# Three feed-forwards rewritten by Strassen's scheme: seven half-size products per pair of weight tiles

## The chip, the core and the metric

The kernel runs on one core of a Trainium2 chip. The time is the device time of the whole program in microseconds (us). Three runs of the kernel before took 4400.33, 4402.57 and 4403.73 us; the median is 4402.57 us.

The engines are called as in the profile: PE is TensorE (the matmuls), DVE is VectorE, ACT is ScalarE, POOL is GpSimd, SP is SyncE, which here only issues DMAs. SBUF is the on-chip memory, PSUM the eight banks that PE writes (one bank holds 128 partitions x 512 fp32), DRAM the chip's large memory.

## The reference

Three blocks work on one sequence of 1024 tokens with 1024 channels. Each has a mixer (recurrences and convolutions, not touched by this change), an output projection, and a feed-forward, all in fp32:

```python
# block 1 (block 3 has the same feed-forward): 4096 hidden channels
h = h + y @ w_out
m = rmsnorm(h, norm_mlp_g) @ w_mlp_up            # 1024 -> 4096
h = h + square(relu(m)) @ w_mlp_down             # 4096 -> 1024
# block 2: 2816 hidden channels, gated
h = h + (silu(m @ w_gate) * (m @ w_up)) @ w_down
```

## The kernel before

Activations lie transposed, channels on the 128 partitions and the 1024 tokens along the free dimension. So `h` is 8 tiles of 128 x 1024, a weight matrix is cut into output tiles of 128 columns, and a hidden layer of 4096 channels is 32 tiles of 128 x 1024 (2816 channels are 22).

**A product in three parts.** PE multiplies in a reduced fp32 form, so each operand is split into an upper part and the rest: `hi` is the rounded copy (made by ACT, `split_hi`, L185) and `lo = x - hi` (made by POOL, `split_lo`, L191, for weights; by DVE for activations). Each product is hi·hi + hi·lo + lo·hi: three matmuls per 128 x 128 piece of weight and 512 tokens. `product` (L220 to L222) makes one output tile: 8 pieces of the contraction x 2 halves of the tokens x 3 = 48 matmuls into two PSUM banks.

**A feed-forward** (`back`, L508) starts with the 8 output tiles of the mixer's projection, whose results are added to `h` (L739), while the norm of the sum is made. It then walks over groups of 8 hidden tiles (`walk`): 8 tiles up, then 8 partial products down, added to `h` at L720. For the up tiles DVE takes the result out of PSUM (L709), scales it by the inverse norm `c_inv` (L712), squares it (L713), and splits it into `pair` (L686, L687), where the down products read it. In block 2 a gate tile and an up tile make one hidden tile (L694 to L702, ACT's Silu at L595). Nothing of the hidden layer goes to DRAM. Loops (`Fori`) run the groups on every engine.

**What sets the order.** Every engine runs its own list of instructions in order; semaphores tie them together. Two weight buffers take turns (`b` = 0, 1): SP loads a tile of 512 KB into `raw` when POOL has split the last one, ACT makes `whi` when PE has finished the product that used the old one, POOL makes `wlo`, PE starts. Tiles of a product use PSUM banks 0 and 1 or 4 and 5.

The function that the change rewrites is `back`, with its helpers `tail_scalar`, `tail_vector` and `sums_of`; `back_half` calls it three times, with `groups` = [(4, 8)] for blocks 1 and 3 and [(2, 8), (1, 6)] for block 2.

Of the kernel before, what the change touches and what calls it, by code (L numbers as in the profile page):

```python
# [15 lines left out]
P = 128  # L16
# [131 lines left out]
MIDDLE = ("m_summed", "m_logged", "m_root", "m_upper", "m_lower", "m_sq_a", "m_tot_a")  # L148
# [106 lines left out]
def next_norm(c, u, gain, off, second=None, of="n"):  # L255

    t = Shared()
    t.of = of
    t.c, t.u, t.gain, t.off, t.second = c, u, gain, off, second
    return t  # L260


def sums_of(pe, s, g, c, how, of="n"):

    for m in range(1 if how == "one" else 2):
        for j in range(2):
            mm = pe.matmul(s.psum[:, 2 + 4 * m + j, :], g.ones[:, :], c.tot[m][:, j * 512:j * 512 + 512], start=True,
                           stop=True)
        mm.then_inc(s[f"{of}_summed"], 1)
# [45 lines left out]


def tail_scalar(act, s, g, t, k):

    h = g.h[:, k, t.off:t.off + SEQ]
    act.wait_ge(s.free[k % 2], t.before + k // 2 + 2)  # L320
    if t.u is not None:
        act.activation(t.u[0][:, k, 0:SEQ], h, ACT.Copy, scale=t.gain(k)).then_inc(s[t.of + "_upper"], 1)
    bufs = len(t.buf_a)
    if k > bufs:
        act.wait_ge(s[t.of + "_tot_a"], k - bufs)
    act.activation(t.c.tot[0][:, 0:SEQ] if k == 0 else t.buf_a[k % bufs][:, 0:SEQ], h, ACT.Square)\
       .then_inc(s[t.of + "_sq_a"], 1)
    if t.second is not None:
        if k > 1:
            act.wait_ge(s[t.of + "_tot_b"], k - 1)  # L330
        act.activation(t.c.tot[1][:, 0:SEQ] if k == 0 else t.buf_b[:, 0:SEQ], h, ACT.Square, scale=t.second(k))\
           .then_inc(s[t.of + "_sq_b"], 1)


def tail_vector(dve, s, g, t, k):

    h = g.h[:, k, t.off:t.off + SEQ]
    if t.u is not None:
        dve.wait_ge(s[t.of + "_upper"], k + 1)
        dve.scalar_tensor_tensor(t.u[1][:, k, 0:SEQ], h, t.gain(k), t.u[0][:, k, 0:SEQ].bitcast(F32), ALU.mult,  # L340
                                 ALU.subtract).then_inc(s[t.of + "_lower"], 1)
    if k == 0:
        return
    sums = [("_sq_a", "_tot_a", t.c.tot[0], t.buf_a[k % len(t.buf_a)])]
    if t.second is not None:
        sums.append(("_sq_b", "_tot_b", t.c.tot[1], t.buf_b))
    for sq, tot, x, buf in sums:
        dve.wait_ge(s[t.of + sq], k + 1)
        if k > 1:
            dve.wait_ge(s[t.of + tot], k - 1)  # L350
        dve.tensor_tensor(x[:, 0:SEQ], x[:, 0:SEQ], buf[:, 0:SEQ], ALU.add).then_inc(s[t.of + tot], 1)
# [156 lines left out]
def back(nc, name, g, c, W, Wup, Wdown, groups, gated, off, middle, end, then=None, early=None, restore=None, ready=0):  # L508
# [11 lines left out]
    with stage(nc, name, *DENSE, *MIDDLE) as s:  # L520
        weight_buffers(s, c)
        xhi, xlo = x
        sq = s.sb("sq", [P, T])
        silu = c.tot[1][:, 0:T] if gated else None
        inv = sliced(g.inv[:, 0:T], T)
        middle.buf_a, middle.before = [c.inv, sq], 0
        end.buf_a, end.buf_b, end.before = [sq], c.inv, total - KD // 2

        def walk(eng, do_up, do_down, skip=0, last_down=None):

            before, tile = outs, 0
            for gi, (many, kt) in enumerate(groups):
                ups = kt if gated else kt // 2
                per = ups + KD // 2

                def one(o, skip=0, final=False):
                    with eng.Fori(0, ups - skip) as j:
                        do_up(j + skip, o * per + before + j + skip, o * kt + tile, kt, o)
                    if final:
                        for j in range(KD // 2):  # L540
                            last_down(j, o * per + before + ups + j, o * kt + tile, kt, o)
                    else:
                        with eng.Fori(0, KD // 2) as j:
                            do_down(j, o * per + before + ups + j, o * kt + tile, kt, o)

                lo, hi = 0, many
                peel = gi == len(groups) - 1 and last_down is not None
                if gi == 0 and skip:
                    one(0, skip)
                    lo = 1  # L550
                if peel:
                    hi -= 1
                if hi - lo > 1:
                    with eng.Fori(0, hi - lo) as o:
                        one(o + lo)
                elif hi - lo == 1:
                    one(lo)
                if peel:
                    one(many - 1, final=True)
                before += many * per  # L560
                tile += many * kt

        with nc.Block() as block:
            @block.sync
            def _(sp):
                def do_up(j, it, tile, kt, o):
                    for b in range(2):
                        at = tile * (2 * P if gated else P) + j * (2 * P) + b * P
                        load_tile(sp, s, b, it, up[:, :, ds(at, P)], KD)

                def do_down(j, it, tile, kt, o):
                    for b in range(2):
                        load_tile(sp, s, b, it, down[:, ds(tile, kt), ds(j * (2 * P) + b * P, P)], kt)

                for it in range(ready, KD):
# [4 lines left out]
                    if it == (1 if early is None else 3) and restore is not None:  # L580
                        sp.dma_start(g.h[:, :, off:off + SEQ], restore).then_inc(s["spilled"], 16)
                for b in range(2):
                    load_tile(sp, s, b, outs, first_up(b), KD)
                walk(sp, do_up, do_down, skip=1)
                if then is not None:
                    for n in range(4):
                        load_tile(sp, s, n % 2, total + n // 2, then(n), KD)
                    for b in range(2):
                        sp.wait_ge(s.landed[b], 16 * total + 32)

            @block.scalar
            def _(act):
                def gate(j, it, tile):
                    act.wait_ge(s["free0"], it + 2)
                    act.activation(silu, silu, ACT.Silu).then_inc(s["silu0"], 1)  # L595

                def do_up(j, it, tile, kt, o):
                    for b in range(2):
                        split_hi(act, s, b, it, KD)
                    if gated:  # L600
                        gate(j, it, tile)

                def do_down(j, it, tile, kt, o):
                    for b in range(2):
                        split_hi(act, s, b, it, kt)

                def last_down(j, it, tile, kt, o):
                    for b in range(2):
                        split_hi(act, s, b, it, kt)
                        if j:  # L610
                            tail_scalar(act, s, g, end, 2 * j - 2 + b)
# [10 lines left out]
                roots_of(act, s, c, "one", "m")  # L622
                if gated:
                    gate(0, outs, 0)
                walk(act, do_up, do_down, skip=1, last_down=last_down)
                tail_scalar(act, s, g, end, KD - 2)
                if then is not None:
                    split_hi(act, s, 0, total, KD)
                tail_scalar(act, s, g, end, KD - 1)
                if then is not None:  # L630
                    split_hi(act, s, 1, total, KD)
# [3404 lines left out]
```

## Time and profile before

| | us |
|---|---|
| median of three runs | 4402.57 |
| span of the profiled execution, first to last instruction | 4393.7 |
| what the runs take beyond that span | 8.9 |
| PE busy in the span | 3927.2 |
| DVE busy | 2089.7 |
| ACT busy | 1119.0 |
| POOL busy | 869.4 |
| DMA, mean of 73 GB/s | 319.75 MB |

No separate time is given for the profiled execution, so the median stands for its span with what lies around it. A PE matmul counts as busy for 0.39 us though the next one starts 0.23 us later, so PE's busy share says only where it had no work; how fast it goes is read from the count of matmuls in a window. The feed-forwards of blocks 1, 2 and 3 lie at about 515 to 1215, 2150 to 2870 and 3675 to 4370 us of the span.

### The profile page before, as it was taken

To read this page: it belongs to the slowest core of one execution; us is meant where nothing else is said; L and a number is where in the kernel's file an instruction comes from. 1 tells how busy PE (TensorE), PEld (TensorE's weight loads), DVE (VectorE), ACT (ScalarE), POOL (GpSimd) and SP (SyncE) were. 2 spreads that over 40 slices of the span, in tenths; PEclk is the share of its full clock that TensorE was granted. 3 is DMA by queue.
4 is the path that set the end of the run, shared out by engine and by line. 5 is a ranking of instruction groups with operands and counts; after the bars stand their busy time and mean duration, and the time that the engine had idled before them with its cause. 6 is when DMAs were issued, how large, how long until landed. Compare 5 with 4: busy or idle time off the path is not lost. (4 is left out here: it accounts for less than half of the span.)

```text
span 4393.7 us, 47463 instructions
## 1 busy us (share of the span) xinstructions
PE 3927.2 (89%) x18690; PEld 3275.1 (75%) x18690; DVE 2089.7 (48%) x2012; ACT 1119.0 (25%) x1368; POOL 869.4 (20%) x653
## 2 busy tenths in 40 slices
PE   9965999999989986767999999999943979999997
PEld 8953888888878776655888888878733958888886
DVE  3677445254544556365331322444768545253353
ACT  2503200000222233244211111243154552000001
POOL 1110222222222210200222222222220512222221
PEclk9987999999999998878999999999967989999998
DMA  3310111111133322442111111122272531111111
GB/s 131 103 45 23 46 51 49 48 48 48 48 130 110 117 80 46 120 156 67 46 50 48 48 48 48 48 82 91 88 177 39 158 126 48 48 48 48 48 50 60
DMA packets 446784, 319.75 MB, mean 73 GB/s; under 512 B 100181, under 2 KB 411989, under 8 KB 446649
## 3 DMA queue, kind: packets, MB, share of 16 engines
q1 hardware_dynamic: 437288, 283.72, 22.0%
q10 hardware_dynamic: 9360, 34.21, 2.0%
q8 instruction: 86, 1.41, 0.1%
q14 instruction: 50, 0.40, 0.0%
HBM read 245.22 MB, written 72.66 MB: 72 GB/s over the span
## 5 line engine op out<-in xcount | busy, mean ns | idle before, releaser
L191 POOL TENSOR_TENSOR c_wlo<-c_raw,c_whi 128x1024 fp32r<-128x1024 f32 (+1 forms) x169 | 409.4, 2423 | 1457.9 <-ACT c_whi L185 1457.9
L220 PE MATMUL c_acc<-c_hi,c_whi 128*128 128x512 f32 x1616 | 633.6, 392 | 0.6 <-POOL c_wlo L191 0.6
L221 PE MATMUL c_acc<-c_lo,c_whi 128*128 128x512 f32 x1616 | 629.2, 389 | 0.0
L222 PE MATMUL c_acc<-c_hi,c_wlo 128*128 128x512 f32 x1616 | 629.2, 389 | 0.0
L191 POOL TENSOR_TENSOR w_wlo<-w_raw,w_whi 128x1024 fp32r<-128x1024 f32 x116 | 291.6, 2514 | 1163.6 <-ACT w_whi L185 1163.6
L220 PE MATMUL c_acc<-pair,c_whi 128*128 128x512 f32 x1120 | 438.1, 391 | 45.6 <-POOL c_wlo L191 45.6
L185 ACT ACTIVATE c_whi<-c_raw 128x1024 fp32r<-128x1024 f32 (+1 forms) x169 | 177.1, 1048 | 1112.5 <-PE c_acc L222 1109.3
L221 PE MATMUL c_acc<-pair,c_whi 128*128 128x512 f32 x1120 | 437.5, 391 | 0.0
L222 PE MATMUL c_acc<-pair,c_wlo 128*128 128x512 f32 x1120 | 437.4, 391 | 0.0
L220 PE MATMUL c_acc<-c_hi,w_whi 128*128 128x512 f32 x1024 | 405.5, 396 | 12.4 <-POOL w_wlo L191 12.4
L221 PE MATMUL c_acc<-c_lo,w_whi 128*128 128x512 f32 x1024 | 399.7, 390 | 0.0
L222 PE MATMUL c_acc<-c_hi,w_wlo 128*128 128x512 f32 x1024 | 399.5, 390 | 0.0
L220 PE MATMUL c_acc<-pair,w_whi 128*128 128x512 f32 (+2 forms) x1024 | 377.4, 369 | 20.6 <-POOLq L165 20.6
L221 PE MATMUL c_acc<-pair,w_whi 128*128 128x512 f32 (+2 forms) x1024 | 373.8, 365 | 0.0
L222 PE MATMUL c_acc<-pair,w_wlo 128*128 128x512 f32 (+2 forms) x1024 | 373.6, 365 | 0.0
L185 ACT ACTIVATE w_whi<-w_raw 128x1024 fp32r<-128x1024 f32 x116 | 122.9, 1059 | 911.3 <-PE c_acc L222 877.6
L220 PEld LDWEIGHTS c_acc<-c_hi,c_whi 128*128 128x128 f32 x1616 | 303.7, 188 | 66.4 <-issue 3.0
L221 PEld LDWEIGHTS c_acc<-c_lo,c_whi 128*128 128x128 f32 x1616 | 303.6, 188 | 64.7 <-issue 2.2
L222 PEld LDWEIGHTS c_acc<-c_hi,c_wlo 128*128 128x128 f32 x1616 | 303.6, 188 | 63.4
L720 DVE TENSOR_TENSOR h<-h,c_acc 128x1024 f32 x64 | 78.2, 1222 | 566.0 <-PE c_acc L222 566.0
L220 PEld LDWEIGHTS c_acc<-pair,c_whi 128*128 128x128 f32 x1120 | 211.4, 189 | 91.2 <-POOL c_wlo L191 47.3
L221 PEld LDWEIGHTS c_acc<-pair,c_whi 128*128 128x128 f32 x1120 | 211.5, 189 | 44.0
(592 smaller groups left out, 5858.7 us busy)
## 6 DMA issues: line engine op xcount, KB each, us to landing
c_raw<-in_w_ff SPq DMA_DIRECT2D x64, 512.0 KB, 4.0
proj<-c_tot ACTq DMA_DIRECT2D x49, 512.0 KB, 2.6
w_raw<-in_w_in SPq DMA_DIRECT2D x48, 512.0 KB, 4.4
c_raw<-in_w_gu SPq DMA_DIRECT2D x44, 512.0 KB, 3.8
w_raw<-in_w_mlp_up SPq DMA_DIRECT2D x32, 512.0 KB, 4.0
w_raw<-in_w_mlp_down SPq DMA_DIRECT2D x32, 512.0 KB, 4.0
h<-proj SPq DMA_DIRECT2D x25, 512.0 KB, 5.7
c_raw<-in_w_in SPq DMA_DIRECT2D x25, 512.0 KB, 4.0
```

The source lines that it names most:

```text
L185: act.activation(s.whi[b][:, 0:kt, :], raw[:, 0:kt, :], ACT.Copy).then_inc(s.hi[b], 1)
L191: pool.tensor_tensor(s.wlo[b][:, 0:kt, :], raw[:, 0:kt, :], s.whi[b][:, 0:kt, :].bitcast(F32), ALU.subtract).then_inc(s.lo[b], 1)
L220: pe.matmul(out, s.whi[b][:, k, :], x_hi, start=(k == 0), stop=False)
L221: pe.matmul(out, s.whi[b][:, k, :], x_lo, start=False, stop=False)
L222: mm = pe.matmul(out, s.wlo[b][:, k, :], x_hi, start=False, stop=(k == kt - 1))
L720: dve.tensor_tensor(h, h, flat(s.psum[:, 4 * b:4 * b + 4, :], T), ALU.add)\
```

## The change

The scheme, in Winograd's form, takes two weight tiles A (cut into quarters: two halves of the contraction, two output tiles) and two halves of the tokens, and makes four output quarters from seven products of half the contraction instead of eight. The seven weight factors are A11, S2, S3, S1, A12, S4, A22 with sums S1 to S4 made by DVE per pair (`weight_sum`); the seven activation operands are three quarters as they are and four sums (T). One *unit* is seven *products* of 12 matmuls (4 pieces of the contraction x 3 parts, 512 tokens each), so 84 matmuls where 96 stood. The results are combined as they leave PSUM: `r1` is the first product, `u2` = r1 + the second, `u3` = u2 + the third, and the quarters C11, C12, C21, C22 from those and from the sums in the banks.

- The feed-forward runs in two passes: all the up units, then all the down units. The first pair of up tiles is still made by plain products (96 matmuls). Blocks 1 and 3 then have 15 up and 16 down units; block 2 has 21 up units (each a gate and an up tile) and 12 down units, the last four with 3 pieces of contraction in place of 4 (63 matmuls).
- Between the passes the hidden layer lies in DRAM, as seven operands per pair of tiles (`hidden`, 7 stores of 256 KB per pair). DVE makes the three sums (`sums_of_hidden`, L978 to L984), SP issues the stores (L608). Before DVE overwrites the place of C22 in the next tile it waits for all seven stores (`kept`).
- The down pass works in chunks of 4 pairs of hidden tiles (four units each). The seven operands of a chunk, 1 MB each, are loaded over the old ones as soon as these are done with, then split by ACT (L755) and DVE (L1102), at the places listed in `REFILL`.
- Weights are split per product: four slots of 128 x 512, ACT at L643, POOL behind it. A pair of weight tiles is loaded as two DMAs of 512 KB with rows of 1 KB.
- The loops are written out, and the ends of the feed-forward (squares and sums for the next norm) are placed among the last four units.

The core of the diff (the engine is the word ahead of each wait: `sp`, `act`, `pool`, `pe`, `dve`; `n` is the unit, `i` the product in it, `r` its place in the order):

```diff
+FACTOR = ("A11", "S2", "S3", "S1", "A12", "S4", "A22")
+BANK = (0, 1, 2, 3, 0, 3, 2)
+REFILL = (3, 4, 6, 8, 9, 11, 12)
...
+            for i in range(7):
+                at = -4 if i == 0 and fetched[nth] else REFILL[i]
+                refill_at.setdefault(divmod(7 * n + at, 7), []).append((nth, i))
...
+                        if r == 2 and n <= NA and (not gated or n % 2):
+                            sp.wait_ge(s["tee"], 4 * pair + 4)
+                            for i in range(7):
+                                sp.dma_start(hidden[i, pair], stored[i]).then_inc(s["kept"], 16)
...
+                        if nth is not None and not (r == 0 and fetched[nth]) and not (r == 6 and nth == 0):
+                            sp.wait_ge(s["fin"], 7 * n + r + 1)
+                            refill(nth, r)
...
+                def split_factor(q):
+                    if q >= 4:
+                        act.wait_ge(s["fin"], q - 3)
...
+                    act.activation(slots[q % 4][:, 0:depth(n), :], factor(n, i), ACT.Copy).then_inc(s["phi"], 1)
...
+                        if q + 4 < 7 * N:
+                            split_factor(q + 4)
...
+                        for nth, i in refill_at.get((n, r), ()):
+                            act.wait_ge(s[f"op{i}"], 16 * nth + 16)
+                            act.activation(hi[:, 0:kk, :], F(lo[:, 0:kk, :]), ACT.Copy).then_inc(s["op_hi"], 1)
...
+                    pool.wait_ge(s["phi"], q + 1)
+                    pool.tensor_tensor(slot[:, 4:4 + kk, :], factor(n, i), F(slot[:, 0:kk, :]), ALU.subtract)\
+                        .then_inc(s["plo"], 1)
...
+                    if i == 4:
+                        pe.wait_ge(s["first"], n + 1)
+                    elif i == 5:
+                        pe.wait_ge(s["c22"], n + 1)
+                    elif i == 6:
+                        pe.wait_ge(s["u3"], n + 1)
...
+                    if begins(n):
+                        pe.wait_ge(s["op_lo"], 7 * chunk(n) + i + 1)
+                    for k in range(kk):
+                        pe.matmul(out, slot[:, k, :], hi[:, k, :], start=fresh and k == 0, stop=False,
+                        pe.matmul(out, slot[:, k, :], lo[:, k, :], start=False, stop=False, skip_group_check=not fresh)
+                        mm = pe.matmul(out, slot[:, 4 + k, :], hi[:, k, :], start=False, stop=k == kk - 1,
...
+                    if i == 3:
+                        dve.wait_ge(s["kept"], 112 * (tile if not gated else tile // 2))
+                        dve.wait_ge(s["u3"], n + 1)
+                        tt(y, r1[:, :], bank(n, 3), ALU.add).then_inc(s["c22"], 1)
...
+                        for nth, j in refill_at.get((n, r), ()):
+                            dve.wait_ge(s["op_hi"], 7 * nth + j + 1)
+                            tt(lo[:, 0:kk, :], F(lo[:, 0:kk, :]), F(hi[:, 0:kk, :]), ALU.subtract)\
+                                .then_inc(s["op_lo"], 1)
```

**Place 1: ACT where a feed-forward goes down.** Before, ACT's list in a loop of up tiles and the loop of down tiles behind it; one row of the loop is two weight tiles of a half product each.

```order
L537 ISA
L185 ACTIVATE w_whi<-w_raw 128x1024 x2
L537 REGISTER_ALU
L537 COMPARE_AND_BRANCH
L543 UNCONDITIONAL_BRANCH
L543 ISA
L185 ACTIVATE w_whi<-w_raw 128x1024 x2
```

Now, ACT's list in block 1 in the first down unit. L643 splits the factor for four products later, L755 splits an operand of the chunk (the fourth to the seventh operand here), L721 copies the first product, L750 is the last square of the hidden layer.

```order
L721 ACTIVATE ff_r<-c_acc 128x512
L643 ACTIVATE w_wlo<-w_raw 128x512
L750 ACTIVATE c_hi_2653<-c_hi_2653 128x512
L643 ACTIVATE w_whi<-w_raw 128x512
L755 ACTIVATE pair<-pair 128x2048
L643 ACTIVATE w_wlo<-w_raw 128x512
L755 ACTIVATE c_hi<-c_lo 128x4x512
L643 ACTIVATE w_whi<-c_tot 128x512
L643 ACTIVATE w_wlo<-ff_sq 128x512
L755 ACTIVATE c_hi<-c_lo 128x4x512
L643 ACTIVATE w_whi<-c_tot 128x512
L755 ACTIVATE c_hi<-c_lo 128x4x512
```

Each L755 stands behind an L643, which waits for a product to end; the operands of a chunk are split among the products of the chunk's own first unit.

**Place 2: DVE between two up tiles of block 1.** Before, the work on one up tile:

```order
L709 TENSOR_SCALAR ff_sq<-c_acc 128x1024
L712 TENSOR_TENSOR ff_sq<-ff_sq,c_inv 128x1024
L713 TENSOR_TENSOR ff_sq<-ff_sq 128x1024
L686 ISA
L686 COPY pair<-ff_sq 128x1024
L687 ISA
L687 TENSOR_TENSOR pair<-ff_sq,pair 128x1024
```

Now, from the last eviction of one unit to C22 of the next (`c_hi_2653` and `c_lo_2654` are fp32 views of `c_hi` and `c_lo`; L1035 and L1043 are C21 and its scaling, L978 to L984 the sums of the hidden layer, L1077 and L1085 `u2` and `u3`, L913 and L916 sums of the next weights, L1019 C22):

```order
L1035 TENSOR_TENSOR c_hi_2653<-c_lo_2654,c_acc 128x512
L1043 SCALAR_TENSOR_TENSOR c_hi_2653<-c_hi_2653,c_inv 128x512
L978 TENSOR_TENSOR c_lo_2654<-c_hi_2653 128x512
L980 TENSOR_TENSOR c_lo_2654<-c_hi_2653,c_lo_2654 128x512
L982 TENSOR_TENSOR c_hi_2653<-c_hi_2653 128x512
L1077 TENSOR_TENSOR c_lo_2654<-ff_r,c_acc 128x512
L984 TENSOR_TENSOR c_lo_2654<-c_hi_2653,c_lo_2654 128x512
L1085 TENSOR_TENSOR ff_r<-c_lo_2654,c_acc 128x512
L913 TENSOR_TENSOR ff_sq<-c_tot 128x512
L916 TENSOR_TENSOR ff_sq<-ff_sq,c_tot 128x512
L1019 TENSOR_TENSOR c_hi_2653<-ff_r,c_acc 128x512
```

The last sum (L984) now stands two products ahead of C22 (L1019), and the seven stores go out between the two.

## Rows read from the trace of the kernel before

**Rows 1.** The page: span, and busy time of each engine.

```profile
span 4393.7 us, 47463 instructions
...
PE 3927.2 (89%) x18690; PEld 3275.1 (75%) x18690; DVE 2089.7 (48%) x2012; ACT 1119.0 (25%) x1368; POOL 869.4 (20%) x653
```

**Rows 2.** Windows; PE, PEld, DVE, ACT, POOL busy (count), then PE clock, DMA share, GB/s.

```profile
560.00:1120.00 560.00, 560.00 (x2472) 463.72 (x2471) 238.72 (x162) 54.12 (x51) 122.32 (x51) 1.00 0.17 49
2200.00:2840.00 640.00, 640.00 (x2825) 529.93 (x2824) 192.11 (x130) 93.95 (x92) 140.53 (x60) 1.00 0.16 48
3700.00:4350.00 650.00, 650.00 (x2869) 538.22 (x2868) 278.36 (x185) 70.03 (x66) 143.97 (x60) 1.00 0.16 47
```

**Rows 3.** Timeline, end of one 48-matmul product: start us, duration us, engine, instruction.

```profile
608.73 0.39 PE L220 MATMUL c_acc<-pair,w_whi 128*128 128x512 f32 x1
...
608.99 1.06 ACT L185 ACTIVATE w_whi<-w_raw 128x1024 fp32r<-128x1024 f32 x1 [9.82 <-PE c_acc L222]
609.07 1.22 DVE L720 TENSOR_TENSOR h<-h,c_acc 128x1024 f32 x1 [2.84 <-PE c_acc L222]
```

**Rows 4.** Timeline, VectorE and GpSimd, up phase of feed-forward 1.

```profile
577.48 2.40 POOL L191 TENSOR_TENSOR w_wlo<-w_raw,w_whi 128x1024 fp32r<-128x1024 f32 x1 [8.47 <-ACT w_whi L185]
577.64 3.33 DVE L712 TENSOR_TENSOR ff_sq<-ff_sq,c_inv 128x1024 f32<-128x1024 f32 x1
...
581.00 1.23 DVE L713 TENSOR_TENSOR ff_sq<-ff_sq 128x1024 f32<-128x1024 f32 x1
```

**Rows 5.** Timeline, GpSimd and VectorE in block 3, VectorE reading PSUM.

```profile
3233.55 2.35 POOL L3072 TENSOR_TENSOR gp_E<-gp_E,gp_bias 128x1024 f32<-128x1024 f32 x1
3234.51 1.28 DVE L3199 TENSOR_TENSOR gp_AT<-gp_dots,gp_E 128x512 f32<-128x512 f32 x2
```

**Rows 6.** Groups by shape: busy us, mean ns of one, then idle before and its releaser.

```profile
L191 POOL TENSOR_TENSOR c_wlo<-c_raw,c_whi 128x1024 fp32r<-128x1024 f32 x161 | 394.6, 2451 | 1402.8 <-ACT c_whi L185 1402.8
...
L712 DVE TENSOR_TENSOR ff_sq<-ff_sq,c_inv 128x1024 f32<-128x1024 f32 x64 | 206.9, 3233 | 2.2
...
L185 ACT ACTIVATE c_whi<-c_raw 128x1024 fp32r<-128x1024 f32 x161 | 170.3, 1058 | 1078.3 <-PE c_acc L222 1075.1 <-POOLq L172 3.2
...
L191 POOL TENSOR_TENSOR c_wlo<-c_raw,c_whi 128x768 fp32r<-128x768 f32 x8 | 14.8, 1852 | 55.1 <-ACT c_whi L185 55.1
...
L3199 DVE TENSOR_TENSOR gp_AT<-gp_dots,gp_E 128x512 f32<-128x512 f32 x16 | 10.5, 685 | 15.6 <-ACT gp_E L2962 9.3 <-PE gp_dots L3104 6.3
...
L2947 ACT ACTIVATE flat<-gp_turn 128x2048 f32<-128x2048 f32 x4 | 7.5, 1878 | 6.8 <-PE gp_turn L3113 6.7
```

**Rows 7.** DMA issues: count, KB each, median us from issue to landing.

```profile
proj<-c_tot ACTq DMA_DIRECT2D x49, 512.0 KB, 2.6
...
w_raw<-in_w_mlp_up SPq DMA_DIRECT2D x32, 512.0 KB, 4.0
...
kept<-h SPq DMA_DIRECT2D x2, 4096.0 KB, 15.1
...
gd_qc<-gp_QD SPq DMA_DIRECT2D x16, 256.0 KB, 5.0
```

**Rows 8.** Timeline of SP's issues: start, duration of the issuing, count.

```profile
3406.79 2.73 SPq L3366 DMA_DIRECT2D gs_qc<-gd_qc  x6
```

**Rows 9.** Timeline at the start of block 2's input layer, after a wait.

```profile
1235.17 2.34 POOL L191 TENSOR_TENSOR w_wlo<-w_raw,w_whi 128x1024 fp32r<-128x1024 f32 x1 [19.59 <-ACT w_whi L185]
...
1237.56 0.80 PE L220 MATMUL c_acc<-c_hi,w_whi 128*128 128x512 f32 x1 [5.07 <-POOL w_wlo L191]
```

**Rows 10.** Windows around that wait, columns as in rows 2.

```profile
1234.73:1238.14 3.41, 0.58 (x1) 0.50 (x2) 3.41 (x2) 1.65 (x2) 2.34 (x1) 0.88 0.00 0
1238.14:1241.55 3.41, 3.41 (x11) 2.67 (x10) 3.41 (x4) 0.00 (x0) 0.00 (x0) 0.62 0.56 155
1241.55:1244.97 3.42, 3.42 (x17) 2.81 (x16) 3.42 (x4) 0.00 (x0) 0.00 (x0) 1.00 0.01 3
```

More of the change, by code:

```diff
@@ L252, in chain_of @@
         yield c
[L255 to L269, printed above, removed]
 def roots_of(act, s, c, how, of="n"):
@@ L314, in scaled_rows @@
            .then_inc(s["n_whole"], 1)
[L317 to L351, printed above, removed]
 def dense(nc, name, g, c, W, tiles, T, u, store=None, conv=None, spill=None, beside=None, off=0, ready=0, then=None,
@@ L519, in back @@
     how = "one" if then is None else "two"
-    with stage(nc, name, *DENSE, *MIDDLE) as s:
-        weight_buffers(s, c)
[L522 to L561, printed above, removed]
@@ new lines, in back @@
+    R = many // 2
+    chunks = [(r, min(4, R - r)) for r in range(0, R, 4)]
+    NA = (many if gated else R) - 1
+    N = NA + 4 * len(chunks)
+    home = ["spare" if (len(chunks) - 1 - n) % 2 and n else "own" for n in range(len(chunks))]
+    fetched = [n > 0 and home[n] != home[n - 1] for n in range(len(chunks))]
+    order = lambda n: FINAL if n == N - 1 else USUAL
+    products = lambda n, i: 7 * n + order(n).index(i) + 1
+    in_up = lambda n: n < NA
+    chunk = lambda n: (n - NA) // 4
+    depth = lambda n: 4 if in_up(n) else chunks[chunk(n)][1]
@@ new lines, in back, with refills @@
+    begins = lambda n: n >= NA and (n - NA) % 4 == 0
+    def refills(n):
+        if n == NA - 1:
+            return 0
+        nth = chunk(n) + 1
+        return nth if n >= NA and (n - NA) % 4 == 3 and nth < len(chunks) else None
+    refill_at = {}
+    for n in range(N):
+        nth = refills(n)
+        if nth is not None:
+            for i in range(7):
+                at = -4 if i == 0 and fetched[nth] else REFILL[i]
+                refill_at.setdefault(divmod(7 * n + at, 7), []).append((nth, i))
@@ L591, in _ @@
             @block.scalar
             def _(act):
[L593 to L611, printed above, removed]
+                def split_factor(q):
+                    n, i = q // 7, order(q // 7)[q % 7]
+                    what = FACTOR[i]
+                    if q >= 4:
+                        act.wait_ge(s["fin"], q - 3)
+                    else:
+                        act.wait_ge(s.done[q // 2], outs + 2)
+                    if what[0] == "A":
+                        act.wait_ge(*landed(n))
+                    else:
+                        act.wait_ge(s["ssum"], 4 * n + int(what[1]))
+                    act.activation(slots[q % 4][:, 0:depth(n), :], factor(n, i), ACT.Copy).then_inc(s["phi"], 1)
@@ L621, in _ @@
                 split_hi(act, s, 1, outs, KD)
[L622 to L626, printed above, removed]
-                if then is not None:
[L628 to L631, printed above, removed]
+                act.wait_ge(s.done[1], outs + 1)
```

583 lines of the change are left out of this document (482 added, 101 removed).

## The prediction, made before the changed kernel ran

> **What bounds the kernel now.** First the page [rows 1]: PE is busy in 89% of the span, DVE in 48%. Then windows inside the feed-forwards [rows 2]: PE has work in all of 560, 640 and 650 us, at full clock. The count gives its pace: 560 us / 2472 = 0.2265 us a matmul (2825 in 640 and 2869 in 650 give the same). The feed-forwards are bound by PE, and each matmul less is worth 0.2265 us as long as nothing else ends later. In the same windows DVE is busy for 30 to 43%, POOL for 22%, and DMA moves 49 GB/s: they have room on average. The question is what PE must wait for between short products.
>
> **What goes.** Blocks 1 and 3: before 64 half-group products x 48 = 3072 matmuls; now 96 + 31 units x 84 = 2700, so 372 fewer each. Block 2: 66 x 48 = 3168 before; now 96 + 29 x 84 + 4 x 63 = 2784, so 384 fewer. Together 1128 x 0.2265 = **-255 us**. The rest of PE's work stays.
>
> **The beat of the new kernel.** A product is 12 x 0.2265 = 2.72 us, a unit 19.0 us. What follows on a product's end starts late: the next product's first matmul began at 608.73, ACT at 608.99 and DVE at 609.07 [rows 3], so 0.26 and 0.34 us. Durations, from [rows 6]: ACT 0.85 us at 768 and 1.06 at 1024 elements, so about 0.64 at 512, and 1.88 at 2048. POOL 1.85 at 768 and 2.4 at 1024 [rows 4], so 1.3 at 512. DVE 0.685 at 512 and 1.22 at 1024 (the undisturbed L713 [rows 4]); another 1024 elements are 1.07 more, so 2.29 at 2048.
>
> DVE and POOL get in each other's way: L712, two inputs in SBUF, began 0.16 us after POOL and ended 1.09 us after POOL's end, 3.33 us in place of 1.23 [rows 4]; its mean over 64 is 3.23 [rows 6]. With one input in PSUM, two DVE operations took 1.28 us together under POOL's operation [rows 5]: not held up. Now POOL works in every product, 1.3 of 2.72 us, so a DVE operation on SBUF that follows an eviction waits for it, about 1.3 us once per product. DVE's list of an up unit is 6 operations from PSUM and 11 on SBUF, 17 x 0.69 = 11.7 us; with seven waits of up to 1.3 it is at most 20.9, about a unit. A down unit has 13, 8.9 to 18 us. So the average still fits, and PE's own factors (split four products ahead, 0.26 + 0.64 + 1.3 = 2.2 us of work in 8.2) are hidden. Three things aren't.
>
> **1. Waiting for the stores (+103 us).** C22 may be evicted only when the seven stores of the tile before have landed, and product 5 (the sixth) needs its bank. Let t = 0 be the end of product 0. DVE evicts u2 after product 1, say at F: 0.34 + 0.69, then waits out POOL to 2.2, last sum to 2.9. SP then issues: each store costs 2.73 / 6 = 0.46 us [rows 8]. A store of 512 KB lands in 2.6 us and one of 4096 KB in 15.1 [rows 7]: 12.5 us for 3.67 MB more, 3.4 us per MB, and 0.8 fixed; seven stores are 1.84 MB, so 6.2 + 0.8 = 7.1 us. Both these rows had other traffic beside them; 256 KB with short rows took 5.0. I take 6.5, so they land at F + 9.4, C22 is out at F + 10.1. Product 5 wants it at F + 3 x 2.72 = 8.2, plus a restart of 0.05 (PE started 0.05 us after POOL's end [rows 9]): a stall of 2.0, say 2.1. Bounds: 0.5 (stores in 5 us) and 5 (stores as slow as 1.3 us apiece). It comes in 30 up units of blocks 1 and 3: 63 us. In block 2 a pair is stored every second unit, 10 times, and a 1024-element product with the gate (1.22 us and its wait for POOL) stands before the sums, so the last sum is about 2 us later: 4 each (2 to 7), 40 us.
>
> **2. Splitting the operands of a chunk (+187 us).** This is the largest term. `REFILL` puts the split of operands 0 to 6 at places 3, 4, 6, 8, 9, 11, 12 counted from the last unit before the chunk; product i of the new unit is place 7 + i. A place is entered when its own product has ended. So operands 5 and 6 are begun only when the product right ahead of their own has ended, and PE has nothing to do: 0.26 to ACT, 0.64 for the factor that stands ahead, 1.88 for the copy, 0.1, 2.29 on DVE, 0.05: 5.2 us each, 10.4 a chunk. Operands 3 and 4 have one product (2.72 us) of cover, but on DVE they stand behind the evictions and sums of their place: at place 8, u2, POOL and two additions to 3.6, then 2.29 = 5.9, so 3.2 late; at place 9 four operations (2.8), POOL 1.3, then 2.29, begun after the last, so 3.0 to 4 late. Operand 2 is up to 1.5 late, since DVE carries 2.29 x 3 extra in that unit. Sum 10.4 + 3.2 + 3.0 + 0.4 = 17 us, x 11 chunks (4, 3, 4) = 187. Bounds: 13 (POOL never in the way) and 24 (POOL between each two, and with the first DVE instruction behind the stores). The loads of 1 MB aren't the limit: at 3.4 us per MB they keep nearly to a product's beat, and they are used seven or more products after they are issued. What was there before at this place, splits of two tiles per 21.8 us of PE, cost nothing.
>
> **3. Starts and ends (+50 us).** After the plain pair DVE must make four activation sums (16 additions of 512, 11 us, and four splits of 2.29), while ACT makes four copies of 1024 and four of 2048, 11.7 us, before it can split factor 2. PE's cover from the projection's last product is two plain tiles, 21.8 us. The lists end at 28 to 31 us, so 5 late, and then C22 waits for stores that leave late: 5 more. I take 10 us a feed-forward, 30. At the end the last rows' squares and sums (two ACT squares of 1.06 and two DVE sums of 1.22 per row, two rows) come after the last product, and the last units carry such sums in DVE's full places: 20 in all. Bounds 20 and 100.
>
> **4. Clock (+26 us).** After PE had idled 5.07 us it worked at the low level: 11 matmuls in 3.41 us where 17 is full [rows 9, 10], the next window was full again. A 5.2 us gap is as long. I charge one product at 0.42 us a matmul instead of 0.2265, 12 x 0.2 = 2.4 us, per chunk: 26. Bounds 0 and the third rival.
>
> **Sum.** -255 + 103 + 187 + 50 + 26 = +111 us on the span of 4393.7: 4505. With the 8.9 us that the runs take beyond it, 4513.6, say **4515 us** against the median of 4402.6: slower by 2.5%. Bounds of the terms all at one end give -255 + 35 + 143 + 20 = -57 and -255 + 220 + 264 + 100 + 187 = +516; neither is likely as a whole.
>
> **A rule against the row.** The pace of 0.2265 us is read from 2472 matmuls. By the Trainium skill ("TensorE: Matmul & The Clock Gate", Back-to-back issue gap) a stream of 512-column matmuls with weight loads runs at about 131 ns each; then a removed matmul would be worth 131 ns, the saving 148 us, and the time 107 us more than I say. The form of the matmul stays, so the row decides and the rule gets no chance.
>
> **Rivals.**
> - *PE keeps the gain (faster).* Only operands 5 and 6 are exposed, and the stores land before C22's place. It decides at stores under 5 us from the last sum and operands 3 and 4 within 2.72 us of their place. For it: DVE and POOL are far from full on average [rows 2]. Against: the order of the lists. 4402.6 - 255 + 11 x 10.4 + 30 + 20 = 4312; with partly covered terms up to 4395. Chance 0.17.
> - *DVE and POOL become the bound.* In up units all of DVE's 11.7 and POOL's 9.2 us run one after the other, and 24 handovers at 0.1 us make 23.3 instead of 19.0: 4.3 x 51 up units = 219 in place of term 1. 4515 + 116 = 4630. For it: the hold-up of every L712; against: evictions from PSUM go on [rows 5]. Chance 0.11.
> - *The clock stays low around each chunk.* Then seven products of each boundary cost 2.4 us more, 17 x 11 = 187 instead of 26: 4675. For it: the row after the 5.07 us gap [rows 10]; against: it recovered within a window. Chance 0.08. The Trainium skill ("TensorE: Matmul & The Clock Gate", HAM oscillation) tells of a kernel whose every block starts on the low clock since PE waits ahead of it; by that rule this rival would hold.
> - Forecast 0.60; the last 0.04 is for what I have not thought of, half to each side.
>
> **Numbers.** The forecast's own range is 4420 to 4610. Out to the rivals I give 4330 to 4650; a third of the first and half of the third lie outside. About 0.2% (9 us) is what runs of this kernel can tell from no change. Faster by more: 0.17 and 0.01 = 0.18; within: 0.02; slower: 0.80.
>
> **What would show it.** Matmuls 17562 in the span. In windows of up units PE at 84 in about 21 us, with one gap before the sixth product, ended by DVE L1019, which itself waits for DMA. PE idle on DVE L1102 the largest item of the waits, 11 x 4 to 5 times, the longest near 5 us. L1102 near 2.3 us, longer when POOL was first. PE clock below full at chunk boundaries. I am wrong if PE's waits on L1102 sum to under 100 us, or those on L1019 to under 30.

## The result, and the profile after

The changed kernel takes **4536.6 us** (median of 4 runs, 4530.6 to 4540.4), the kernel before 4401.5 in the runs beside it: ratio 1.0308, 95% interval 1.0293 to 1.0322. It is slower by 3.1%; the prediction was 4515, 2.5%. The profiled execution took 4538.75 us with a span of 4536.7, so the span grew by 143.0 us. The page, as [rows 1]:

```profile
span 4536.7 us, 47120 instructions
...
PE 3799.0 (84%) x17562; PEld 3124.9 (69%) x17562; DVE 2810.1 (62%) x3066; ACT 1620.2 (36%) x2163; POOL 1433.8 (32%) x1128
```

PE has the 17562 matmuls that were forecast, 1128 fewer. Its busy time fell by 128 us and not by 255, mostly because matmuls at the low clock take longer. The windows, as [rows 2], for the up and the down phase of each feed-forward:

```profile
560.00:820.00 260.00, 249.12 (x1081) 202.46 (x1081) 190.95 (x217) 91.21 (x154) 137.67 (x90) 1.00 0.41 141
820.00:1240.00 420.00, 355.67 (x1439) 286.13 (x1438) 269.80 (x269) 151.73 (x185) 187.54 (x120) 0.92 0.36 122
2240.00:2700.00 460.00, 417.62 (x1729) 339.91 (x1728) 326.97 (x340) 130.19 (x191) 204.77 (x145) 0.94 0.30 104
2700.00:2950.00 250.00, 210.40 (x838) 168.23 (x838) 150.74 (x160) 83.64 (x110) 105.95 (x75) 0.90 0.30 98
3820.00:4080.00 260.00, 248.47 (x1071) 201.75 (x1071) 188.92 (x218) 91.01 (x154) 135.73 (x88) 0.99 0.40 137
4080.00:4490.00 410.00, 347.82 (x1403) 279.66 (x1402) 256.30 (x259) 140.09 (x173) 186.08 (x117) 0.91 0.36 126
```

Where before PE had work in every microsecond, it now idles for 4% of an up phase of blocks 1 and 3, 9% of block 2's, and 15 to 16% of the down phases; the granted clock is 0.94 in block 2's up phase and 0.90 to 0.92 in the down phases. The waits name the two places (us in all, times, longest):

```profile
PE c_acc L831 <- DVE c_lo L1102: 112.9, 29, 4.9
PE c_acc L831 <- DVE c_hi L1019: 89.0, 41, 9.8
...
PE c_acc L831 <- DVE pair L1102: 42.8, 13, 6.1
...
DVE c_hi L1019 <- DMA hidden<-c_lo: 125.6, 39, 6.1
```

L1102 is the split of a chunk's operand: 155.7 us in all. L1019 evicts C22, and it waits for the stores (the last row: DVE's own wait).

**A split without a lead.** Timeline of the changed kernel, feed-forward 1, first unit of the first chunk: product 4 ends, product 5 begins (start us, duration us, engine, instruction, idle before):

```profile
875.37 0.39 PE L834 MATMUL c_acc<-c_hi,w_wlo 128*128 128x512 f32 x1
875.79 0.63 ACT L643 ACTIVATE w_wlo<-ff_sq 128x512 fp32r<-128x512 f32 x1 [2.10 <-PE c_acc L834]
875.79 0.69 DVE L1054 TENSOR_TENSOR h<-h,c_acc 128x512 f32<-128x512 f32 x1 [1.45 <-PE c_acc L834]
876.33 1.89 ACT L755 ACTIVATE c_hi<-c_lo 128x2048 fp32r<-128x2048 f32 x1
...
878.25 2.29 DVE L1102 TENSOR_TENSOR c_lo<-c_lo,c_hi 128x2048 fp32r<-128x2048 f32 x1 [1.77 <-ACT c_hi L755]
...
880.69 0.77 PE L831 MATMUL c_acc<-c_hi,w_whi 128*128 128x512 f32 x1 [4.94 <-DVE c_lo L1102]
...
881.68 0.63 PE L834 MATMUL c_acc<-c_hi,w_whi 128*128 128x512 f32 x1
```

This is the predicted chain link by link: ACT's factor 0.63, the copy 1.89, the split 2.29. From the end of one product's 12 matmuls to the next one's first (the last start and one pace, 875.37 + 0.23, to 880.69) PE stands for 5.1 us; 5.2 was forecast. Then the matmuls take 0.63 us and start 0.42 apart. The windows of product 5, the gap behind it, and product 6 (the clock is the third column from the end):

```profile
880.69:885.75 5.06, 5.06 (x12) 3.81 (x12) 0.00 (x0) 0.00 (x0) 0.00 (x0) 0.50 0.00 0
885.75:891.09 5.34, 0.41 (x2) 0.03 (x1) 3.58 (x3) 2.43 (x2) 1.71 (x1) 0.82 0.00 0
891.09:896.16 5.07, 5.07 (x12) 4.01 (x13) 0.00 (x0) 0.00 (x0) 0.00 (x0) 0.50 0.01 3
```

Both products run wholly at 0.50, the level of 1.2 GHz, 5.06 us in place of 2.72, and the clock comes back up only while PE waits for the next.

**The stores.** Timeline of feed-forward 1, unit 2: the last sum, SP's first store, C22, product 5.

```profile
591.97 0.69 DVE L984 TENSOR_TENSOR c_lo<-c_hi,c_lo 128x512 f32<-128x512 f32 x1
...
592.68 0.34 SPq L608 DMA_DIRECT2D hidden<-c_hi  x1
...
599.39 0.69 DVE L1019 TENSOR_TENSOR c_hi<-ff_r,c_acc 128x512 f32<-128x512 f32 x1 [2.23 <-DMA hidden<-c_lo]
...
600.23 0.47 PE L831 MATMUL c_acc<-c_hi,w_wlo 128*128 128x512 f32 x1 [0.74 <-DVE c_hi L1019]
```

The seven stores take 6.7 us from the first issue (6.5 forecast), yet PE loses 0.9 us here and not 2.1: the last sum follows its eviction at once (591.97), since POOL's next operation began 0.11 us after it and not ahead. In the 28 up units of blocks 1 and 3 the gap is 0.9 us in the median and 37.3 in all: two units stand out with 4.8 and 4.5 us, the last of each up phase, where the seven stores are issued between the first loads of the down phase and take 10.5 and 10.2 us to land. In block 2 the gap is 3.4 to 3.7 us in every second unit (4 forecast).

**The account.** The trace holds the start of each matmul, so each product of 12 (or 9) gives a gap ahead of it and its time above 0.2265 us a matmul. Summed by place, in us:

| place | gaps | low clock |
|---|---|---|
| first unit of a chunk (11): product 3 / 4 / 5 / 6 | 42.2 / 7.9 / 55.3 / 56.0 (with product 2: 164.9) | 66.8 |
| up units, product 5 | 73.0 (all: 74.4) | 26.9 |
| first unit of a feed-forward (3) | 26.9 | 8.1 |
| last three units (3 x 3), other | 9.9 | 2.7 |
| sum | 276.1 | 104.5 |

-255.5 + 276.1 + 104.5 = 125.1; the last 17.9 of the 143.0 lie ahead of product 0, behind the last product, and in the rest of the program; they were not taken apart.

The first chunk of each feed-forward is dearer than the others, 17.2 to 19.3 us of gaps against 13.3 to 14.3: the gap ahead of its product 3 is 6.3 to 6.5 us where the others have 2.7 to 3.0. ACT's and DVE's lists still hold the end of the up phase there.

### The profile page after: what moved, and what is told of

Read it like the earlier page. It is cut to its first block and busy times, and to the rows that moved or that the text cites. A ratio compares the mean times of both kernels' runs of the same rounds, so it can differ in the third digit from the quotient of the medians.

```text
span 4536.7 us, 47120 instructions
## 1 busy us (share of the span) xinstructions
PE 3799.0 (84%) x17562; PEld 3124.9 (69%) x17562; DVE 2810.1 (62%) x3066; ACT 1620.2 (36%) x2163; POOL 1433.8 (32%) x1128
## 3 DMA queue, kind: packets, MB, share of 16 engines
q8 instruction: 140, 2.29, 0.2%
## 5 line engine op out<-in xcount | busy, mean ns | idle before, releaser
L788 POOL TENSOR_TENSOR c_whi<-c_tot,c_whi 128x512 fp32r<-128x512 f32 (+1 forms) x132 | 197.9, 1499 | 346.7 <-ACT c_whi L643 346.7
L788 POOL TENSOR_TENSOR c_wlo<-c_raw,c_wlo 128x512 fp32r<-128x512 f32 (+1 forms) x124 | 199.5, 1609 | 190.3 <-ACT c_wlo L643 190.3
L831 PE MATMUL c_acc<-c_hi,c_whi 128*128 128x512 f32 x420 | 179.9, 428 | 78.9 <-DVE c_hi L1019 40.7
L831 PE MATMUL c_acc<-c_hi,c_wlo 128*128 128x512 f32 x412 | 171.5, 416 | 60.7 <-DVE c_lo L1102 37.5
L831 PE MATMUL c_acc<-pair,c_whi 128*128 128x512 f32 x466 | 187.6, 403 | 27.1 <-DVE pair L1102 25.8
L219 PE MATMUL c_acc<-c_hi,w_whi 128*128 128x512 f32 x480 | 193.0, 402 | 12.4 <-POOL w_wlo L190 12.4
L219 PE MATMUL c_acc<-pair,w_whi 128*128 128x348 f32 (+1 forms) x512 | 177.1, 346 | 20.6 <-POOLq L164 20.6
L643 ACT ACTIVATE c_whi<-c_tot 128x512 fp32r<-128x512 f32 (+1 forms) x132 | 82.2, 623 | 304.0 <-PE c_acc L834 304.0
L220 PE MATMUL c_acc<-c_lo,w_whi 128*128 128x512 f32 x480 | 188.1, 392 | 0.0
L221 PE MATMUL c_acc<-c_hi,w_wlo 128*128 128x512 f32 x480 | 187.9, 392 | 0.0
L833 PE MATMUL c_acc<-pair,c_whi 128*128 128x512 f32 x466 | 185.8, 399 | 0.0
L834 PE MATMUL c_acc<-pair,c_whi 128*128 128x512 f32 x466 | 185.2, 397 | 0.0
L833 PE MATMUL c_acc<-c_lo,c_whi 128*128 128x512 f32 x420 | 176.8, 421 | 0.0
L834 PE MATMUL c_acc<-c_hi,c_whi 128*128 128x512 f32 x420 | 176.5, 420 | 0.0
L220 PE MATMUL c_acc<-pair,w_whi 128*128 128x348 f32 (+1 forms) x512 | 173.6, 339 | 0.0
```

Source lines behind the costliest of these rows:

```text
L219: pe.matmul(out, s.whi[b][:, k, :], x_hi, start=(k == 0), stop=False)
L220: pe.matmul(out, s.whi[b][:, k, :], x_lo, start=False, stop=False)
L221: mm = pe.matmul(out, s.wlo[b][:, k, :], x_hi, start=False, stop=(k == kt - 1))
L643: act.activation(slots[q % 4][:, 0:depth(n), :], factor(n, i), ACT.Copy).then_inc(s["phi"], 1)
L788: pool.tensor_tensor(slot[:, 4:4 + kk, :], factor(n, i), F(slot[:, 0:kk, :]), ALU.subtract)\
L831: pe.matmul(out, slot[:, k, :], hi[:, k, :], start=fresh and k == 0, stop=False, skip_group_check=not fresh)
```

## The experiments

All times are medians of 4 runs beside runs of the kernel before (4398 to 4400 us in each set). "Chunk gaps" (those in the first unit of each chunk, 164.9 us in the changed kernel) and "low clock" are from the account above, made again for each kernel.

**1 and 2. Other places for the splits.** One line is changed:

```
-REFILL = (3, 4, 6, 8, 9, 11, 12)
+REFILL = (4, 5, 6, 7, 8, 9, 10)      # even
+REFILL = (3, 4, 5, 7, 8, 10, 11)     # one_earlier
```

> REFILL = (4, 5, 6, 7, 8, 9, 10): each operand of a chunk is split two whole products ahead of its use, where the leads were 3, 3, 2, 1, 1, 0, 0. Theory (the waits at their places, and the low clock behind them): two products are 5.4 us, the chain ACT and DVE 5.2, so of the 15.0 us of gaps per chunk the two of 5.1 go and the 4.2 ahead of the fourth product shrinks; 4 to 6 us a chunk are left, from DVE's own evictions. -110 us of gaps, -35 of low clock: 4390 to 4440 us, and PE's wait on L1102 falls from 156 to under 70. Rival (DVE with POOL is the bound, the place of a split doesn't matter): the gaps only move, 4500 to 4570. Rival (the loads of 1 MB are late): the split starts when the load lands, and DVE or ACT waits for DMA; gain under 60.

> REFILL = (3, 4, 5, 7, 8, 10, 11): leads of 3, 3, 3, 2, 2, 1, 1 products. Theory: operands 5 and 6 have 2.7 us of cover against a chain of 5.2, so they still cost about 2.5 each, operand 3 little: 7 us a chunk in place of 15, -85 us of gaps and -30 of clock, about 4425, between the run with even leads and the changed kernel. Rival (DVE with POOL bound): no change, 4500 to 4570.

*even*: 4427.0 us, ratio 1.0063 (1.0045 to 1.0082). *one_earlier*: 4419.7, ratio 1.0054 (1.0038 to 1.0071). The same instructions at other places are worth 110 and 117 us, so the rival that the place doesn't matter is out. Waits of *even*:

```profile
PE c_acc L831 <- DVE h L1051: 33.5, 15, 3.5
PE c_acc L831 <- DVE c_lo L1102: 29.7, 16, 3.2
PE c_acc L831 <- DVE pair L1102: 22.1, 16, 4.3
```

L1102 fell from 155.7 to 51.8, as expected, but an eviction, L1051, came up: DVE is now late with its whole list. Chunk gaps are 86.8 and not about 55; *one_earlier* has 79.1 (86 fewer, 85 expected), though not where it was expected: 1.4, 2.3 and 3.2 us ahead of products 3, 4 and 5, and 0.15 ahead of 6. The rival that the loads of 1 MB are late holds at one place only: in *even* ACT waits for a load once in each feed-forward, for operand 6 of the first chunk (6.7 to 7.9 us), and PE's gaps ahead of that product are 2.0, 3.4 and 2.0 us. In the changed kernel ACT never waits for these loads.

**3. Stores.** The store that C22's place needs goes first, with a semaphore of its own; the other six follow in an order of their own (0, 3, 1, 2, 4, 5, 6 without that one) and are waited for one eviction later:

```
+                            sooner = 2 if gated else 5
+                            sp.dma_start(hidden[sooner, pair], stored[sooner]).then_inc(s["kept_a"], 16)
...
-                        dve.wait_ge(s["kept"], 112 * (tile if not gated else tile // 2))
+                        dve.wait_ge(s["kept_a"], 16 * (tile if not gated else tile // 2))
...
                     if i == 4:
+                        dve.wait_ge(s["kept"], 96 * (tile if not gated else tile // 2))
```

> The one store that C22's place needs is issued first, with a semaphore of its own; C22 waits for that alone, the other six stores are waited for one eviction later. Theory (store wait with its low clock, 73 + 25 us in up units, 10 at each start): it lands 5 us sooner, so PE's waits on L1019 go nearly to zero: -70 to -110 us, 4430 to 4465; most of it in block 2, where the gaps were 3.5 each. Rival (DVE is late by its own list, the store only the last of two): DVE ends C22 hardly sooner, gain under 30 us, 4505 or more.

4431.9 us, ratio 1.0078 (1.0062 to 1.0095): 105 us. The gaps of the up units go from 74.4 to 2.6, their low clock from 26.9 to 0.9; C22's line on DVE in this kernel, with the idle time before it, against 128.0 in the changed one:

```profile
L1023 DVE TENSOR_TENSOR c_hi<-ff_r,c_acc 128x512 f32<-128x512 f32 x51 | 34.5, 677 | 5.7 <-DMA hidden<-c_hi 3.3 <-PE c_acc L838 2.4
```

And in a stretch of up units PE has work all the time, 220 / 972 = 0.2263 us a matmul, with DVE busy for 77% of it:

```profile
560.00:780.00 220.00, 220.00 (x972) 182.16 (x971) 170.11 (x198) 81.13 (x139) 120.59 (x82) 1.00 0.43 148
```

So in up units neither DVE nor POOL is the bound, though both work beside PE. The gaps at chunks stay (170.2 against 164.9).

**4. Filler.** While PE waits it multiplies into a bank that is overwritten later:

```
                     if begins(n):
+                        filler = {3: 12, 5: 20, 6: 20}.get(i, 0)
+                        if filler:
+                            pe.wait_ge(s["c12"], n)
+                            pe.wait_ge(s["c22"], n)
+                            for m in range(filler):
+                                pe.matmul(bank(n + 1, 3), slot[:, m % kk, :], moving(n, 0)[0][:, m % kk, :], start=True, stop=True)
```

> Nothing is moved; while PE waits for operands 3, 5 and 6 of a chunk it multiplies 12, 20 and 20 matmuls into a bank that the next product but one overwrites from fresh. They fill 2.7 and 4.5 of the gaps of about 4.2, 5.1 and 5.1 us. Theory (66.8 us of the loss at chunks is the low clock that the idle time brings): the gaps stay, the products behind them run at 2.72 instead of 5.05 us: -40 to -60 us, 4475 to 4497, and the granted clock goes from 0.915 to about 0.94. Rival (the slow products are not from idling, or the gap starts when the product before has ended whatever the clock): 4535 or more, since the filler can only delay.

4496.1 us, ratio 1.0217 (1.0198 to 1.0236): 41 us faster with 572 matmuls more. The timeline of its PE at products 5 and 6 of the first chunk:

```profile
879.73 3.56 PE L832 MATMUL c_acc<-c_hi,w_whi 128*128 128x512 f32 x15
883.60 0.50 PE L837 MATMUL c_acc<-c_hi,w_whi 128*128 128x512 f32 x1 [0.30 <-DVE c_lo L1108]
886.49 4.70 PE L832 MATMUL c_acc<-c_hi,w_wlo 128*128 128x512 f32 x20
891.51 0.50 PE L837 MATMUL c_acc<-c_hi,w_wlo 128*128 128x512 f32 x1 [0.32 <-DVE c_lo L1108]
```

From 883.60 to 886.49 product 5 is done at full pace, with a granted clock of 1.00 where the changed kernel had 0.50. The time that PE can't use (filler and idle) is still 5.0 us a product; low clock at chunks went from 66.8 to 15.8. So the slow products come from PE's idling. The gap ahead of product 4 grew from 7.9 to 22.2, about what product 3 became faster by (its low clock went from 18.8 to 5.1): a product at the low clock also covers up to 2.3 us more of the next operand's chain.

**5. POOL's share.** POOL makes the lower half of the weight factors for 16 of 128 columns, so part of the work is left out:

```
-                    pool.tensor_tensor(slot[:, 4:4 + kk, :], factor(n, i), F(slot[:, 0:kk, :]), ALU.subtract)\
+                    pool.tensor_tensor(slot[:, 4:4 + kk, 0:16], factor(n, i)[:, :, 0:16], F(slot[:, 0:kk, 0:16]), ALU.subtract)\
```

> POOL's lower halves of the weight factors are made for 16 of 128 columns alone (the rest of that part keeps old numbers); else it is the changed kernel. The page of the changed kernel has a DVE operation on SBUF of 512 elements at 1.60 us beside POOL's work, against 0.68 from PSUM. Theory (PE waits for stores and for splits of 2.3 us, not for DVE's sum of work): DVE's busy time falls by 200 us and more but the time only by 10 to 50 us, through the last sums ahead of the stores: 4490 to 4525. Rival (DVE and POOL on one port are the bound): 100 us or more, under 4435.

4456.6 us, ratio 1.0130 (1.0113 to 1.0146): 80 us, more than my 10 to 50 and less than the rival's 100. DVE's busy time fell by 273 us. The line that shows it, first in the changed kernel, then here:

```profile
L1043 DVE SCALAR_TENSOR_TENSOR c_hi<-c_hi,c_inv 128x512 f32<-128x512 f32 x90 | 122.0, 1356 | 3.1
```

```profile
L1043 DVE SCALAR_TENSOR_TENSOR c_hi<-c_hi,c_inv 128x512 f32<-128x512 f32 x90 | 71.8, 798 | 3.1
```

The Trainium skill ("SBUF — State Buffer", SBUF: two separate sides) says that VectorE with two SBUF inputs and GpSimd take a shared port pair as an exclusive lock; this pair of rows agrees. The changed kernel's splits show it instruction by instruction, here one in the second chunk:

```profile
962.46 2.28 DVE L1102 TENSOR_TENSOR pair<-pair 128x2048 fp32r<-128x2048 f32 x1
963.02 2.86 POOL L788 TENSOR_TENSOR w_wlo<-w_raw,w_wlo 128x512 fp32r<-128x512 f32 x1 [1.04 <-ACT w_wlo L643]
```

POOL's operation takes 1.26 to 1.31 us with no VectorE operation beside it. The 30 that begin alone inside a split of 2048 elements, 0.34 to 1.44 us after its start, all end 1.13 to 1.16 us behind the split's end. In five cases POOL was first; the split then ends 2.15 us after POOL's end and takes 2.77 to 2.79 us in place of 2.28 to 2.29.

By the account the gaps of the up units fell from 74.4 to 47.5, of the first units from 26.9 to 15.2, of the last three from 9.2 to 2.8, and the low clock there by 20; at chunks, product 3 fell from 42.2 to 32.1; but product 5 of a chunk has 55.0 (55.3) and product 6 has 55.9 (56.0). POOL makes the waits longer where DVE's list leads to them, ahead of C22 and of operand 3. It is neither the bound nor in the chain of operands 5 and 6.

**6. Both edits (3 and one_earlier).**

> The store that C22 needs first with its own semaphore, and REFILL = (3, 4, 5, 7, 8, 10, 11). Theory (two separate waits): the gains of the two edits add, 4536 - 105 - 117 = 4315 us (4300 to 4335), faster than the kernel before by 2%; the 255 us of removed matmuls are then nearly all on PE's path but for about 80 us of gaps and 37 of low clock at chunks. Rival (one shared limit, DVE with POOL, under both): the second gain is under half, 4370 or more.

**4313.4 us**, ratio 0.9800 (0.9784 to 0.9816): faster than the kernel before by 2.0%. 4536.6 - 105 - 117 = 4315, so the two waits add. The waits of PE and, from the timeline, DVE at product 3 to 5 of the second chunk:

```profile
PE c_acc L835 <- DVE c_lo L1107: 56.0, 24, 5.2
```

```profile
925.45 2.78 DVE L1107 TENSOR_TENSOR pair<-pair 128x2048 fp32r<-128x2048 f32 x1
928.15 0.68 DVE L1082 TENSOR_TENSOR c_inv<-ff_r,c_acc 128x512 f32<-128x512 f32 x1
928.87 2.76 DVE L1069 TENSOR_TENSOR h<-h,c_inv 128x512 f32<-128x512 f32 x2
931.55 2.28 DVE L1107 TENSOR_TENSOR c_lo<-c_lo,c_hi 128x2048 fp32r<-128x2048 f32 x1
933.75 0.68 DVE L1090 TENSOR_TENSOR ff_r<-c_inv,c_acc 128x512 f32<-128x512 f32 x1
...
937.97 2.28 DVE L1107 TENSOR_TENSOR c_lo<-c_lo,c_hi 128x2048 fp32r<-128x2048 f32 x1
940.17 0.68 DVE L1059 TENSOR_TENSOR h<-h,c_acc 128x512 f32<-128x512 f32 x1
941.04 2.51 DVE L1107 TENSOR_TENSOR c_lo<-c_lo,c_hi 128x2048 fp32r<-128x2048 f32 x1 [0.19 <-ACT c_hi L759]
```

From 925.45 to 943.55 DVE idles for 0.19 us in 18: here its list is the bound. Its splits of 2.78 and 2.51 us, each begun while POOL was at work and ended 2.1 us behind POOL's end, show that POOL's hold is in that list too; how much of the lateness would go without it was not run. 82.2 us of chunk gaps and 36.1 of low clock are left; 37.0 of the gaps lie in the three first chunks (11.6 to 13.3 us each), 5.1 to 7.7 in each of the other eight.

**7 to 9. What is left at chunks.** *both_c* splits each operand in halves, for ACT and DVE alike; PE waits for the second half ahead of its third row of tiles. *both_b* has that too, with the even places and ACT's copy ahead of its factor. *both_d* is both_a with other places.

```
-                            act.activation(hi[:, 0:kk, :], F(lo[:, 0:kk, :]), ACT.Copy).then_inc(s["op_hi"], 1)
+                            for a, b in ((0, 2), (2, kk)):
+                                act.activation(hi[:, a:b, :], F(lo[:, a:b, :]), ACT.Copy).then_inc(s["op_hi"], 1)
```

> As both_a, and each operand of a chunk is split in two halves of 1024 and 1024 elements: ACT, DVE and PE each start on the first half while the engine ahead is on the second. The chain falls from 1.9 + 2.3 to about 1.0 + 1.2 before the product may begin. Theory: the gaps ahead of products 3 to 6 of a chunk (7.2 us a chunk) fall by 2 to 4: 4270 to 4295 us. Rival (DVE's list in those places is what is late, and halves cost 0.1 us more each): no gain on both_a, 4310 to 4325.

> As both_c, with REFILL = (4, 5, 6, 7, 8, 9, 10), and ACT copies the operand ahead of the factor of its place (the factor has four products of slack). Theory: the copy starts 0.65 us sooner and each operand has two products of lead, so only DVE's list is left: 4260 to 4300, at or under both_c. Rival (with even leads DVE must carry 2.3 us in every product of the unit and falls behind by its end): 5 to 25 us above both_c, as the run with even leads alone was above one_earlier.

> both_a with REFILL = (3, 4, 5, 6, 8, 9, 11): operands 3 and 5 one product sooner than in both_a. In both_a the gaps are 1.3 us ahead of product 3, 2.3 ahead of 4 and 3.1 ahead of 5 per chunk. Theory as it stands now (after the long leads are given, what is left is DVE's list from place 3 on, 7 splits of 2.4 us beside its own 9 to 18 us a unit): the sum of the gaps changes little, 72 to 92 us where both_a has 82, time 4295 to 4325. Rival (each operand is late by its own chain alone): product 5's 34.6 us go, 4265 to 4285.

4315.9, 4322.4 and 4314.3 us; ratios 0.9815 (0.9798 to 0.9831), 0.9824 (0.9807 to 0.9840), 0.9802 (0.9785 to 0.9818). My theory for both_c and both_b was wrong: the chunk gaps are 83.5 and 84.7 where both_a has 82.2. A shorter chain was worth nothing here, as it should be where DVE's sum of work is late. In both_b PE waits for an eviction more than for a split:

```profile
PE c_acc L839 <- DVE h L1060: 46.0, 15, 5.1
...
PE c_acc L839 <- DVE c_lo L1112: 22.6, 12, 2.8
```

both_d was expected from that: product 5's gaps fell from 34.6 to 20.7, those of 4 and 6 rose by 13.0 and 15.8, the sum is 87.8.

**10. both_filled**, 6 and 9 fillers ahead of products 4 and 5 of both_a.

> both_a, with 6 filler matmuls ahead of product 4 and 9 ahead of product 5 of each chunk's first unit, while PE waits for their operands (gaps of 2.3 and 3.1 us on average there, 27.2 us of low clock behind them in all). Theory (low clock comes from the idle time): about 20 of those 27 us come back, less some 5 where the filler outlasts the gap: 4290 to 4305. Rival (gaps of this size bring no low clock by themselves, or the filler delays as much as it saves): 4308 to 4325.

4304.5 us, ratio 0.9784 (0.9767 to 0.9800), the fastest kernel here. Low clock at chunks falls from 36.1 to 10.4; gaps, filler included, rise from 82.2 to 100.2. The intervals of the two ratios overlap, so the gain of some 9 us over both_a is likely and not certain.

**11. later.** The other direction, REFILL = (3, 4, 6, 9, 10, 11, 12) in the changed kernel.

> The changed kernel with REFILL = (3, 4, 6, 9, 10, 11, 12): operands 3 and 4 are split one product later, so with no lead, like 5 and 6. Theory (a split costs its chain, 5.1 us, less 2.72 for each product of lead): the gaps ahead of products 3 and 4 become 5 to 6.5 each, where they are 3.8 and 0.7, and with low clock behind both: +70 to +95 us of gaps and +15 to +30 of clock, 4620 to 4660. Rival (DVE's sum of work sets the pace): the same total in other places, 4530 to 4560.

4645.2 us, ratio 1.0559 (1.0541 to 1.0577), as expected. Gaps ahead of products 3 to 6 in all: 77.0, 55.5, 55.7, 55.7, so 5.05 us each for 4, 5 and 6, and 7.0 for 3, more than my 6.5. Low clock at chunks is 90.4.

## Why the prediction was right, and where its sizes were off

- **What goes**: 1128 x 0.2265 = -255 holds. Once one of the waits is gone, a stretch runs at 0.2263 (experiment 3), and with both cut the kernel is faster (6).
- **Term 2, splits, +187**: 164.9. Operands 5 and 6 cost 5.03 and 5.09 each (5.2), 3 costs 3.8 (3.2): 2.7 to 3.0 in eight chunks and 6.3 to 6.5 in the three first ones, which the sum had not set apart. Operand 4 costs 0.7 and not 3.0: I had added late operands as if each started anew, but while PE stands for operand 3, ACT and DVE go on with 4, and product 3 at the low clock covers more of it. Without that cover, in *filled*, operand 4 costs 2.0.
- **Term 1, stores, +103**: 74.4 in the up units. The stores took what I said; but POOL was already at work in only 5 of the 43 cases when the last sum ahead of them (L984) began, so the gap in blocks 1 and 3 is 0.9 in the median and not 2.1.
- **Term 3, starts and ends, +50**: 26.9 + 9.9 + up to 17.9 = about 54.
- **Term 4, clock, +26**: 104.5, the term that was mis-sized, by a factor of four. I charged one product a chunk. In fact each long gap costs its own: products 3, 5 and 6 of a chunk cost 1.7, 1.9 and 2.1 us, and the up units' waits for stores cost 25 too, 19 of it in block 2, which I had at nothing. Terms 1, 2 and 4 were 316 together and came to 343.8, 28 more; with 4 more of term 3 that is the 32 us by which the span passed the forecast 4505. So splits and stores, 51 us too dear, hid most of the clock, 78 too cheap: that the total came so near is in part luck.
- **The 8.9 us beyond the span**: the runs beside the experiments, of either kernel, take 1.7 to 2.1 us beyond their own span. Most of the 8.9 was the difference between one profiled execution and the median of others, so the time, 4536.6 against 4515, looks 10 us nearer to the forecast than the span does.
- **Rivals.** *PE keeps the gain* failed as argued from [rows 3 to 6]: with no lead the chain is exposed, and operand 3 was late too. *DVE and POOL the bound* is false for the changed kernel (experiments 1 to 3), though POOL's hold on DVE is worth 80 us of it (5); at chunks DVE's list is the bound once the leads are given (6 to 9). *The clock stays low around each chunk* had a right part, more low clock than one product, and a wrong price: 6.1 us a chunk and not 17. The slow products are only those behind a gap. The rule that was named there (the Trainium skill, "TensorE: Matmul & The Clock Gate", HAM oscillation) tells of blocks that start on the low clock behind their wait. The trace agrees for the long waits (1.4 to 2.3 us lost behind each gap of 5 us), and not for the 39 gaps under 2 us (0.1 to 0.2 each). That seven products stay slow was the prediction's own step from it, and the trace does not show it.
- **The other rule** (131 ns a matmul) is not borne out: 972 matmuls in 220 us are 226 ns each with PE busy throughout (3).

Not tried: to take work off DVE at chunks, by weight sums on POOL or by storing both halves of the operands. That would be the next step; nothing here says what it gives.

## What to carry to other kernels

Price a split just ahead of its use by its whole chain over the engines, and give it the lead of that chain first: one line of places was worth 117 us here, and the saving of a cheaper algorithm shows only then. Of several late things in a row count the first, then ask what the others do meanwhile. Beside nearly every gap of 3 us and more on PE stood a second cost here, the product behind it at the low clock; when leads have made the engine's list the bound, only less work on it helps.

## What the hardware showed that I had not expected

- A gap of 5.1 us cost PE another 2.3 us in the product behind it when all of it ran at 1.2 GHz (5.06 in place of 2.72), and an average of 1.9 to 2.1 us. Of all gaps of the changed kernel, the 39 of 0.3 to 2.0 us cost 0.1 to 0.2 each; of the 14 between 2 and 3 us, four cost 0.1 and ten 0.8 to 2.3; of the 40 longer ones, 38 cost 1.4 to 2.3. The ten of 3.4 to 3.7 in block 2 cost 18.9 in all.
- The chip gives the clock back for useless work: 572 matmuls more, 41 us less.
- VectorE's scaling of 512 elements (L1043, both inputs in SBUF) takes 692 ns with no GpSimd operation beside it, 1.61 us in the mean of the 65 that found one under way, and 1356 ns over all 90; with small GpSimd operations the mean is 798.
- In the splits of experiment 5 the second operation waits for the whole of the first, whichever engine it is on: GpSimd's 1.3 us become 2.0 to 3.1 when they begin inside a split of 2.28 us. The 2048-element split itself is held in only 5 of 70 cases. In the first timeline GpSimd's operation had ended at 877.77, ahead of the split.
